# First weight block split into its two column halves, and the last piece of x moved to the SyncE queue

## The reference, cut to what matters

```python
def rmsnorm(x, g):
    xf = x.astype(jnp.float32)
    y = xf * lax.rsqrt(jnp.mean(xf * xf, axis=-1, keepdims=True) + EPS)
    return (y * g.astype(jnp.float32)).astype(x.dtype)

def mlstm_mixer(x, norm_g, w_in, b_gates, h_norm_g, w_out):
    b_, s_, _ = x.shape
    u = rmsnorm(x, norm_g) @ w_in
    q, k, v, o, gi, gf = jnp.split(u, M_SPLITS, axis=-1)
...
def reference(...):
    x = first_block(...)      # mlstm_mixer, conv_ffn, shared_kv, moba_mixer, conv_ffn
    return second_block(x, ...)
```

## Time and profile before

| | before |
|---|---|
| median of 3 runs | 950.68 us |
| the profiled execution, its own time | 950.92 us |
| its span | 949.1 us |
| PE busy | 936.4 us (99%) |
| DVE busy | 800.1 us (84%) |
| ACT busy | 278.1 us (29%) |
| DMA, HBM read and written | 169.69 MB and 2.64 MB, 182 GB/s over the span |
| chain that ended last | PE 92%, DVE 4%, DMA 2%, ACT 1% |

### The profile page before, as it was taken

The page is one execution under the profiler, slowest core; times in us unless marked ns, Lnnn a source line. Parts: engine busy times, 40 slices in busy tenths (PEclk is TensorE's granted clock), DMA queues, the critical chain, the costliest instruction groups (busy, mean ns, idle before and its releaser), DMA issues.

```text
span 949.1 us, 16131 instructions
## 1 busy us (share of the span) xinstructions
PE 936.4 (99%) x6456; PEld 865.3 (91%) x6456; DVE 800.1 (84%) x1822; ACT 278.1 (29%) x622; POOL 0.7 (0%) x7
## 2 busy tenths in 40 slices
PE   8999999999999999999999999999999999999997
PEld 7888999999999988889999999999888878888876
DVE  3778879999998878778699999988799985899953
ACT  1033122221212112263122221220424563624561
POOL 0000000000000000000000000000000000000000
PEclk9999999999999999999999999999999999999999
DMA  8943455464634750657254645447933428443101
GB/s 302 409 183 117 177 180 211 167 244 155 257 145 154 231 215 1 270 210 289 108 223 157 243 170 231 176 156 244 338 132 102 163 90 289 167 146 108 36 1 45
DMA packets 36859, 171.80 MB, mean 181 GB/s; under 512 B 5032, under 2 KB 8880, under 8 KB 23344
## 3 DMA queue, kind: packets, MB, share of 16 engines
q1 hardware_dynamic: 35120, 167.72, 48.0%
q10 hardware_dynamic: 1664, 3.04, 0.9%
HBM read 169.69 MB, written 2.64 MB: 182 GB/s over the span
## 4 chain that ended last, share of the span: by engine, by line
PE 92%; DVE 4%; DMA 2%; ACT 1%; issue 1%; ACTq 0%; SPq 0%; DVEq 0%
PE bank L1354 26%; PE bank L1374 14%; PE bank L1039 9%; PE bank L1457 5%; PE bank L1668 4%; PE bank L1107 3%; PE bank L1572 3%; PE bank L1330 3%; PE bank L1553 3%; PE bank L1300 3%; PE bank L1114 3%; PE bank L1654 3%; PE bank L1050 1%; PE bank L1497 1%; DMA ring<-in_ring 1%; PE bank L1600 1%
## 5 line engine op out<-in xcount | busy, mean ns | idle before, releaser
L1374 PE MATMUL bank<-work,fring 128*128 128x128 f32 x1008 | 115.5, 275 | 0.0
L1374 PEld LDWEIGHTS bank<-work,fring 128*128 128x128 f32 x1008 | 114.0, 192 | 0.0
L2490 DVE SCALAR_TENSOR_TENSOR work<-work,cols 128x256 f32<-128x256 f32 x240 | 98.8, 477 | 1.0 <-ACT work L893 0.5
L1354 PE MATMUL bank<-sq,fring 128*128 128x128 f32 x640 | 84.5, 275 | 0.0
L724 ACT ACTIVATE work<-work,cols 128x256 f32<-128x256 f32 x88 | 47.8, 593 | 110.8 <-DVE work L2213 96.0
L1354 PE MATMUL bank<-ring,fring 128*128 128x128 f32 x640 | 78.1, 275 | 0.0
L1354 PE MATMUL bank<-sq,ring 128*128 128x128 f32 x640 | 78.0, 275 | 0.0
L1354 PEld LDWEIGHTS bank<-sq,fring 128*128 128x128 f32 x640 | 77.9, 192 | 0.0
L1354 PEld LDWEIGHTS bank<-ring,fring 128*128 128x128 f32 x640 | 74.8, 192 | 0.2
L1354 PEld LDWEIGHTS bank<-sq,ring 128*128 128x128 f32 x640 | 74.7, 192 | 0.0
L2232 DVE SCALAR_TENSOR_TENSOR work<-work,cols 128x256 f32<-128x256 f32 x176 | 71.5, 477 | 0.0
(11 more groups left out here) (416 smaller groups left out, 1725.5 us busy)
## 6 DMA issues: line engine op xcount, KB each, us to landing
ring<-in_ring SPq DMA_DIRECT2D x60, 1024.0 KB, 6.9
fring<-in_up SPq DMA_DIRECT2D x44, 1024.0 KB, 6.9
ada_w<-in_ada SPq DMA_DIRECT2D x48, 512.0 KB, 6.3
fring<-in_down SPq DMA_DIRECT2D x44, 512.0 KB, 4.5
ring<-in_ring SPq DMA_DIRECT2D x2, 800.0 KB, 6.7
bias_skewed<-bias_rows SPq DMA_DIRECT2D x1, 1536.0 KB, 12.8
consts<-in_consts ACTq DMA_DIRECT2D x1, 1128.0 KB, 15.1
ring<-in_ring SPq DMA_DIRECT2D x2, 512.0 KB, 4.7
```

The lines of the kernel that those rows point to most:

```text
L1354: last = mm(bank[:, P * at:P * (at + 1)], w[:, k, P * c:P * (c + 1)], x[:, k, :], start=(k == 0), stop=(k == 3))
L1374: last = mm(bank[:, at + P * c:at + P * (c + 1)], w[:, P * c:P * (c + 1)], x, start=(i == 0 and at == 0 and c == 0), stop=(i == FF_STEPS - 1),
L2490: marks[c] = link(v.scalar_tensor_tensor(b_y[:, c, :], b_a[:, c, tap:tap + T], col("conv_w_2", 124 * l + 4 * tap + c), b_y[:, c, :], ALU.m ...
```

## The change

Block 0 is laid out in HBM by its two halves of columns: first all eight chunks of the columns 0 to 127, then all eight chunks of the columns 128 to 255. The first product does the eight chunks of the first half and then the eight chunks of the second. Block 0 now comes in four transfers (`FIRST_W`): 128 KB (first half, chunks 0 and 1), 384 KB (first half, chunks 2 to 7), and 256 KB each for the two parts of the second half. SP issues the first two, then the last piece of x, then the third; ACT issues four pieces of x and the fourth part of the weight.

```diff
+        FIRST_W = ((0, 2 * P), (2 * P, D), (D, D + 4 * P), (D + 4 * P, 2 * D))
...
-            for m, (k0, k1) in enumerate(FIRST):
-                sem = "ring0" if k1 == DC else f"first_w{m}"
-                sp.dma_start(slot(0)[:, 256 * k0:256 * k1], I["ring"][0][:, 256 * k0:256 * k1]).then_inc(S(sem), 16)
+            for m in range(2):
+                a, b = FIRST_W[m]
+                sp.dma_start(slot(0)[:, a:b], I["ring"][0][:, a:b]).then_inc(S(f"first_w{m}"), 16)
+            lo, hi = DC + T * FIRST[4][0], DC + T * FIRST[4][1]
+            sp.dma_start(x_tile[:, lo:hi], I["x"][:, lo:hi]).then_inc(S("piece4"), 16)
+            a, b = FIRST_W[2]
+            sp.dma_start(slot(0)[:, a:b], I["ring"][0][:, a:b]).then_inc(S("first_w2"), 16)
             sp.wait_ge(S("piece3"), 16)
...
-            for m, (k0, k1) in enumerate(FIRST):
+            for m, (k0, k1) in enumerate(FIRST[:4]):
                 lo, hi = (0 if k0 == 0 else DC + T * k0), DC + T * k1
                 act.dma_start(x_tile[:, lo:hi], I["x"][:, lo:hi]).then_inc(S(f"piece{m}"), 16)
+            a, b = FIRST_W[3]
+            act.dma_start(slot(0)[:, a:b], I["ring"][0][:, a:b]).then_inc(S("ring0"), 16)
...
-            for k in range(DC):
-                for m, (k0, k1) in enumerate(FIRST):
-                    if k == k0:
-                        pe.wait_ge(S("ring0" if k1 == DC else f"first_w{m}"), 16)
-                pe.wait_ge(S("xg_ready"), k + 1)
-                for c in range(2):
-                    last = mm(pb[0][:, T * c:T * (c + 1)], slot8(0)[:, k, P * c:P * (c + 1)], xg[:, k, :],
-                              start=(k == 0 and c == 0), stop=(k == DC - 1), skip_group_check=True)
+            for c in range(2):
+                for k in range(DC):
+                    at = D * c + P * k
+                    for m, (a, b) in enumerate(FIRST_W):
+                        if at == a:
+                            pe.wait_ge(S("ring0" if m == 3 else f"first_w{m}"), 16)
+                    if c == 0:
+                        pe.wait_ge(S("xg_ready"), k + 1)
+                    last = mm(pb[0][:, T * c:T * (c + 1)], slot(0)[:, at:at + P], xg[:, k, :],
+                              start=(k == 0), stop=(k == DC - 1))
             last.then_inc(S("product"), 1)
...
+def columns_apart(ring):
+
+    first = ring[0].reshape(P, DC, 2, P).transpose(0, 2, 1, 3).reshape(1, P, -1)
+    return np.concatenate([first, ring[1:]])
...
-        "ring": ring_blocks(g),
+        "ring": columns_apart(ring_blocks(g)),
```

## The result

The changed kernel takes 953.56 us (median of 7 runs, 953.17 to 955.09) against 950.72 us (7 runs): ratio 1.0027, interval 1.0017 to 1.0038, so slower by about a quarter of a per cent. The profiled execution took 953.48 us (span 951.7) against 950.92 (949.1), 2.56 us more.

What follows compares the result with a forecast made beforehand. Two nearly equal paths, DMA with VectorE and TensorE's own, were taken to meet at 26.85 us. TensorE's 1.76 us delay less 0.27 free gave +1.49, so 952.2 us from the median 950.68; range 951.0 to 953.8.

Steps and rivals of the forecast that it cites:

- no change beyond 0.2% (0.72): Whole kernel: chance 0.72 that the time stays within 0.2%, 1.9 us; slower had 0.26, faster 0.02.
- the clock's rival: First product: sparse matmuls let TensorE's clock fall, 0.90 us per matmul instead of 0.43; +2.2 to +4.3 us, chance 0.15.
- one of its own signs: Opening: prediction wrong altogether if x lands over a microsecond off the map, or the delay at 28 us isn't the end's.
- Two paths meeting at 26.85: Third factor's start: DMA and VectorE's path ends at 26.80, TensorE's at 26.58; TensorE delays up to 0.27 us are free.
- Matmuls reordered, TensorE's path +1.76: First product: two matmuls per piece of x instead of four, eight left behind; ends at 15.92 instead of 14.16.
- The second, third and fourth piece at 6.54, 9.03 and 10.25 us: Opening: forecast landings of pieces of x with queues alternating by packet; the fourth 0.6 us late, bounds 0 and 0.8.
- my map from bytes to times: Opening: bytes ahead of each piece of x turned into landing times by the earlier landings, 3.76 to 11.17 us.
- The case named as hidden: First product: x lands some 0.9 us earlier than mapped, product ends near 14.4; +0.0 us (-0.3 to +0.6), chance 0.10.
- The path of DMA and VectorE, +0.8 and hidden: Block 3 and VectorE's sums before the third factor: 0.8 us later, ending at 27.6, hidden behind TensorE's 28.34.
- A delay at the third factor passes on to the end: First factor needing VectorE's sums, started at 26.85: no later chain link at a fixed time, so delay is paid in full.
- the one DMA link that I had named: Chain behind the opening: a 4.11 us transfer at 782 us, issued when VectorE frees a buffer, moves with the rest.
- Nothing for the layout and the transfers of block 0: Block 0: ACT's issue slots stay five, SP issues one transfer less while waiting anyway, layout free on the chip; no cost.

## Why the prediction was right, and where not

The forecast of 952.2 us lay 1.4 us below the measured 953.56, inside its range. Its sign was right, its size 1.5 us against 2.8, and its likeliest statement, no change beyond 0.2% (0.72), didn't come. Two paths were late: the forecast came near the delay of one by luck and had the other wrong. The measured +2.8 lies in the span given to the clock's rival (+2.2 to +4.3), but keeping the clock up gained nothing by itself. And by one of its own signs the prediction fails altogether: x landed more than a microsecond otherwise than mapped.

*Two paths meeting at 26.85.* Shown: holding the constants shortened one path and made TensorE's own the bound, keeping the clock up shortened the other and brought nothing while block 3 was late. That TensorE's path was 0.27 us from the other is true of the one execution only, and by the starts the distance was 0.43 even there.

*Matmuls reordered, TensorE's path +1.76.* Measured +1.86, and the agreement is luck. The order alone, run by itself, cost 1.5 us, its fall of the clock included. In the changed kernel the fourth piece came 1.1 us earlier than forecast (9.11 against 10.25), and the clock fell, which was a rival at 0.15 and costs 1.2 us of TensorE's path in the profile: two errors that cancel. The sign named for that rival, records of 634 ns behind 9 us, is there.

*The second, third and fourth piece at 6.54, 9.03 and 10.25 us.* They landed at 6.41, 7.71 and 9.11. The second is right, the third is 1.3 us early and the fourth 1.1. For these my map from bytes to times took the landings of one execution for a law of the bytes; with unchanged transfers the third piece landed at 8.40, 8.06, 7.61 and 7.50 us in four executions. The case named as hidden had the third piece landing by 7.8 and came true in that, but not in its time, since the order, the clock and the constants each cost more than it allowed. That the queues alternate by packet is borne out by the counts while both have work (50 and 49 from 20 to 22 us). The Trainium skill, DMA: Bandwidth & Descriptors, section Queues, rings and completion order, says as well that an engine changes between queues packet by packet.

*The path of DMA and VectorE, +0.8 and hidden.* This is the step that failed. It was +2.21 and it decided. SP's blocks were forecast 0.6 us later and came 0.55 earlier. I had ScalarE's transfers 0.3 us earlier and priced 0.9 us of its queue, against SP's, at 0.1 MB per us. They were issued 2.0 us earlier (9.14 against 11.17), because the last piece of x now lands with the fourth and releases the last square at once. Against SP's blocks that is a lead of 1.5 us, which at the forecast's rate would be 0.15 MB and 0.4 us. Measured were 1.17 MB and 2.75 us more for block 3, so the rate was the larger error: it was read at a time when ScalarE's queue brought rows of 2 and 3 KB (gate weight and columns), and a lead lets in the constants behind them, in rows of 9 KB (1128 KB over 128 partitions). Where packets alternate, these take half of the bytes beside SP's blocks with their 8 KB rows, and not a quarter as in the earlier trace rows. Both sides are tested: with the constants held back the changed kernel loses 0.08% instead of 0.27, and the kernel before with nothing but this changed loses 0.27%. But the two delays run side by side and don't add up: without the constants TensorE's own path is still late, by the 1.1 us that the kernel with the constants held back loses.

*A delay at the third factor passes on to the end.* Right: 2.21 of the 2.56 us stand there, 0.27 more came at the one DMA link that I had named. That this link adds nothing of its own is not right: it took 4.11 to 6.32 us in the ten executions.

*Nothing for the layout and the transfers of block 0.* Right for the transfers: with the old order they are as good as the kernel before with its constants held back. The layout was not run by itself. The order with it, the new transfers and held constants costs 1.1 us, and without all three 1.5, so these runs show no cost of the layout; one below a microsecond they couldn't tell.

## What to carry to other kernels

When a transfer is moved forward, look at who waited for it and what that engine issues next: the transfers that were moved cost nothing in themselves, but a shorter wait let 1.8 MB of constants loose early, and 1.17 MB of them came ahead of the weights that the critical path wanted. With them held back, 1.1 of the 2.8 us of loss were left, which go to the new order. Where queues alternate by packet, hold back a queue of large rows that nobody needs yet by a wait on a landing; here one line gave 0.16% in the kernel before. Ahead of a stall, put work that doesn't need what is awaited: splitting a product so that less can be done ahead of the gap lengthens the tail behind it, and may cost the clock besides. In the changed kernel's profile the order made TensorE's path 1.4 us longer at full clock, and the fall of the clock 1.2 more.

## What was not expected of the hardware

The clock fell to 0.50 (1.2 GHz) behind a stretch in which TensorE was not idle, but busy 1.29 of 3.30 us, with gaps of 1.32 and 0.69 us; the kernel before had a gap of 2.00 us there and kept its clock. With the order alone it fell after one gap of 2.43 us, and in the wait of 2.45 us of the kernel with early constants. The Trainium skill, TensorE: Matmul & The Clock Gate, Part 1, has the clock set by how busy TensorE has been of late, and puts the lower level down to idle time. In the changed kernel it fell although work stood between the gaps. In one more execution the matmuls kept the pace of the lower level until 14 us, while the column said 1.00; the durations of the records show it and the column does not. The landing of one and the same piece of x varied by 0.9 us between executions, several times the 0.27 us on which the forecast's balance of two paths stood.
